# A two-block kernel on 272 columns: its first stage loads x in pieces, makes the parts of x straight from x, halves two weight slabs, issues zero products first and moves the statistic by some units

## The reference

```python
hn = rms_norm(h, g_mix[0])                      # h: meta tokens and x, 272 x 1024
z = hn @ w_in                                   # 1024 -> 384 + 256 + 32 + 3*512 + 8
c_q, c_kv, k_pe, fq, fk, fv, f_logit = split(z)
q = rms_norm(c_q, g_cq) @ w_uq ; kv = rms_norm(c_kv, g_ckv) @ w_ukv
qf, kf = rms_norm(fq per head, g_q_fox), rms_norm(fk per head, g_k_fox)
cum_log_f = cumsum(log_sigmoid(f_logit + b_forget))
# two attentions (one with cum_log_f as decay), joined @ w_out, then an MLP;
# after it a convolution mixer and MLP, then a second block of two mixers and two FFNs
```

## Time and profile before

| what | us |
|---|---|
| median of 3 runs | 1374.69 (1373.73 to 1377.56) |
| profiled execution, its own time | 1373.33 |
| its span | 1371.6 |
| TensorE busy (matmuls) | 1322.3 (96%) |
| DVE, ACT, POOL busy | 969.3, 735.5, 445.8 |
| first matmul | 12.79 |
| matmul of the statistic | 23.86 |
| first matmul of unit 2 | 24.22 |
| first matmul of unit 18 | 87.44 |
| first matmul of attention | 111.66 |

### The profile page before, as it was taken

One profiled execution on the slowest core, in us unless ns is written; L12 is line 12 of the kernel. 1 busy time (PEld: TensorE's weight loads), 2 busy tenths in 40 slices (PEclk: granted clock), 3 DMA queues, 4 the chain that ended last, 5 costly groups with the idle time before them and its releaser, 6 DMA issues. The chain is left out here.

```text
span 1371.6 us, 29146 instructions
## 1 busy us (share of the span) xinstructions
PE 1322.3 (96%) x10774; PEld 1288.3 (94%) x10774; DVE 969.3 (71%) x1440; ACT 735.5 (54%) x1204; POOL 445.8 (33%) x462
## 2 busy tenths in 40 slices
PE   5999999999999999999999999999999899999996
PEld 5787699999999999999989999999999889999996
DVE  6767567664578677655655569998569798999844
ACT  5454655444444444444455547665445785766642
POOL 3532044321111433311545423333125534343300
PEclk9998999999999999999999999999999999999998
DMA  7440044555545555555534555554554446555451
GB/s 268 166 141 32 1 152 159 184 185 183 184 181 189 180 184 184 185 184 183 205 134 155 185 185 185 183 183 145 201 207 154 154 162 208 185 184 183 147 198 54
DMA packets 34507, 230.52 MB, mean 168 GB/s; under 512 B 3838, under 2 KB 4990, under 8 KB 10662
## 3 DMA queue, kind: packets, MB, share of 16 engines
q1 hardware_dynamic: 33652, 226.47, 47.4%
q10 hardware_dynamic: 770, 2.90, 0.6%
HBM read 228.17 MB, written 1.05 MB: 167 GB/s over the span
## 5 line engine op out<-in xcount | busy, mean ns | idle before, releaser
L365 DVE TENSOR_TENSOR wlo<-raw,whi 128x1024 fp32r<-128x1024 f32 (+1 forms) x448 | 548.2, 1229 | 92.1 <-ACT whi L360 91.0
L400 PE MATMUL ps<-xhi,whi 128*128 128x256 f32 (+2 forms) x2064 | 585.0, 283 | 21.2 <-DVE wlo L365 17.8
L401 PE MATMUL ps<-xlo,whi 128*128 128x256 f32 (+2 forms) x2064 | 583.2, 283 | 0.0
L402 PE MATMUL ps<-xhi,wlo 128*128 128x256 f32 (+2 forms) x2064 | 581.9, 282 | 0.0
L360 ACT ACTIVATE whi<-raw 128x1024 fp32r<-128x1024 f32 (+1 forms) x448 | 448.9, 1009 | 134.1 <-PE ps L402 130.0
L400 PEld LDWEIGHTS ps<-xhi,whi 128*128 128x128 f32 x2064 | 390.2, 189 | 26.5 <-issue 20.8
L402 PEld LDWEIGHTS ps<-xhi,wlo 128*128 128x128 f32 x2064 | 390.9, 189 | 0.0
L401 PEld LDWEIGHTS ps<-xlo,whi 128*128 128x128 f32 x2064 | 388.5, 188 | 0.3
L400 PE MATMUL ps<-hhi,whi 128*128 128x256 f32 (+1 forms) x1184 | 335.2, 283 | 3.3 <-issue 2.6
L402 PE MATMUL ps<-hhi,wlo 128*128 128x256 f32 (+1 forms) x1184 | 334.4, 282 | 0.0
L401 PE MATMUL ps<-hlo,whi 128*128 128x256 f32 (+1 forms) x1184 | 334.2, 282 | 0.0
(11 more groups left out here) (261 smaller groups left out, 1293.2 us busy)
## 6 DMA issues: line engine op xcount, KB each, us to landing
raw<-w SPq DMA_DIRECT2D x184, 1024.0 KB, 4.8
raw<-w SPq DMA_DIRECT2D x40, 768.0 KB, 4.2
h<-x_fm ACTq DMA_DIRECT2D x1, 1088.0 KB, 6.3
out_fm<-h SPq DMA_DIRECT2D x8, 128.0 KB, 2.0
ws<-ws_src ACTq DMA_DIRECT2D x1, 512.0 KB, 4.6
bs<-bs_rows ACTq DMA_DIRECT2D x1, 512.0 KB, 5.4
consts<-constants ACTq DMA_DIRECT2D x1, 508.0 KB, 9.6
q_fox<-decay_rows SPq DMA_DIRECT2D x1, 340.0 KB
```

The costliest lines, as they stand in the source:

```text
L365: nc.vector.tensor_tensor(wlo[:, j % HLR, 0:n], raw[:, slot, col:col + n], whi[:, j % HLR, 0:n].bitcast(F32), ALU.subtract).then_inc(wlo_d ...
L400: nc.tensor.matmul(o, hi, xh, start=start, stop=False)
L401: nc.tensor.matmul(o, hi, xl, start=False, stop=False)
L402: mm = nc.tensor.matmul(o, lo, xh, start=False, stop=stop)
```

## The change

- x is loaded in 4 pieces of two chunks, each with its semaphore. `xhi` of even chunks is made by DVE, of odd chunks by ACT, straight from x times the gain; `xlo` by DVE in one instruction, x\*gain - xhi. `xg` is no longer used here.
- SP loads only the first 88 columns of params at first, the others after the pads (awaited after attention). Slab 0 is loaded in halves, the second issued once piece 1 of x is there; slab 1 in halves once all of x is there; then slab 2, `consts`, slab 3.
- TensorE first issues 46 products of zeros (128x128 by 256 columns, bank 7, operands in `chi`, cleared by DVE), then units 0 and 1 interleaved: hi\*hi and hi\*lo of unit 0, then of unit 1, then lo\*hi of both.
- The 8 squares go to 8 buffers; POOL sums them, after the last `xlo`. The column sum follows unit 4 instead of unit 1; root and reciprocal come at t = 3 and t = 4. ACT runs one Sqrt of a single column at the start.
- The shared tile is unit 4 instead of 0, the fox queries are units 0 to 3. The gate's first DVE steps are at t = 4 (were 1), the Exp at 5 (4), the reciprocal at 7 (5), the scan at 14 (12), the decay rows' DMAs at 16 (14).
- Spreads of the queries follow units 8 and 9 (were 7, 8), of the keys 12 and 13 (11, 12); the norms are at t = 9, 10 and 13, 14, and `inverse(1)` stands ahead of the norms of t = 10. `turn_v` is two groups after unit 14 (or query tile 2) and one a unit (or tile) later.

```diff
+WARM = 46
 # block.sync
-                    body(0, wait=False)
+                    half = UB * P
+                    sp.dma_start(raw[:, 0, 0:half], src[0][:, 0:half]).then_inc(s("unit0_loaded"), 16)
+                    sp.wait_ge(x_loaded[1], 16)
+                    sp.dma_start(raw[:, 0, half:cols], src[0][:, half:cols]).then_inc(raw_full[0], 16)
+                    for i in (0, 2, 3):
+                        sp.wait_ge(x_loaded[i], 16)
+                    sp.dma_start(raw[:, 1, 0:half], src[1][:, 0:half]).then_inc(s("unit2_loaded"), 16)
+                    sp.dma_start(raw[:, 1, half:cols], src[1][:, half:cols]).then_inc(raw_full[1], 16)
+                    sp.dma_start(raw[:, 2, 0:cols], src[2]).then_inc(raw_full[2], 16)
+                    sp.dma_start(consts[:, :], consts_in).then_inc(consts_in_done, 16)
+                    sp.dma_start(raw[:, 3, 0:cols], src[3]).then_inc(raw_full[3], 16)
+                    rest = pcol["conv_w"][0]
+                    sp.dma_start(params[:, rest:npar], params_in[:, rest:npar]).then_inc(s("params_loaded"), 16)
 # block.tensor
-            pe.wait_ge(consts_in_done, 16)
+            pe.wait_ge(s("warm_set"), 1)
+            for _ in range(WARM):
+                nc.tensor.matmul(ps[:, 7, 0:SEQ], chi[:, 0, 0:P], chi[:, 0, 0:SEQ], start=True, stop=True)
-                if u == 1:
+                if u == 4:
+                    pe.wait_ge(consts_in_done, 16)
+            def first_units():
+
+                o = [ps[:, take(), 0:T0] for _ in range(2)]
+                for u in range(2):
+                    pe.wait_ge(whi_done, u + 1)
+                    for b in range(8):
+                        if u == 0 and b % 2:
+                            pe.wait_ge(xhi_done, b + 1)
+                        elif u == 0:
+                            pe.wait_ge(xg_done, b + 2)
+                        nc.tensor.matmul(o[u], whi[:, u, b * P:(b + 1) * P], xhi[:, b, :], start=b == 0, stop=False)
+                    for b in range(8):
+                        if u == 0:
+                            pe.wait_ge(xlo_done, b + 1)
+                        nc.tensor.matmul(o[u], whi[:, u, b * P:(b + 1) * P], xlo[:, b, :], start=False, stop=False)
+                for u in range(2):
+                    pe.wait_ge(wlo_done, u + 1)
+                    for b in range(8):
+                        mm = nc.tensor.matmul(o[u], wlo[:, u, b * P:(b + 1) * P], xhi[:, b, :], start=False,
+                                              stop=b == 7)
+                    mm.then_inc(unit_done, 1)
+
+            first_units()
+            for u in range(2, U_KN):
-                if u in (7, 8):
+                if u in (8, 9):
                     for i in (0, 1):
-                        spread(0, 2 * (u - 7) + i, take_ring())
-                if u in (11, 12):
+                        spread(0, 2 * (u - 8) + i, take_ring())
+                if u in (12, 13):
                     for i in (0, 1):
-                        spread(1, 2 * (u - 11) + i, take_ring())
-                if u == 13:
-                    turn_v(1)
+                        spread(1, 2 * (u - 12) + i, take_ring())
+                if u == 14:
+                    turn_v(1, (0, 1))
+                if u == 15:
+                    turn_v(1, (2,))
-                    turn_v(0)
+                    turn_v(0, (0, 1))
+                if x == 3:
+                    turn_v(0, (2,))
 # block.vector
+            nc.vector.memset(chi[:, 0, :].bitcast(F32), 0.0).then_inc(s("warm_set"), 1)
+            for i in range(2):
+                first_xhi(2 * i)
+                first_xlo(2 * i)
+                first_xlo(2 * i + 1)
+            first_xhi(4)
+            first_xhi(6)
+            for kt in range(4, KT):
+                first_xlo(kt)
+            for j in range(LA):
                 split_lo(dve, 0, j, 8)
-            for kt in range(KT):
-                dve.wait_ge(sq_done, kt + 1)
-                dve.wait_ge(ssum_done, kt + 1)
-                nc.vector.tensor_tensor(ssum[:, :], ssum[:, :], sq[:, kt % 2, :], ALU.add).then_inc(ssum_done, 1)
-                if t in (8, 9):
-                    for i in (0, 1):
-                        fox_normed(0, 2 * (t - 8) + i)
                 if t == 10:
                     inverse(1)
+                if t in (9, 10):
+                    for i in (0, 1):
+                        fox_normed(0, 2 * (t - 9) + i)
+                if t == TL_PE:
+                    dve_rstd(dve, 0, 0, T0)
 # block.scalar
+            for i in range(4):
+                act.dma_start(h[:, 2 * i:2 * i + 2, :], x_in[:, 2 * i:2 * i + 2, :]).then_inc(x_loaded[i], 16)
+            act.wait_ge(s("warm_set"), 1)
+            nc.scalar.activation(four[:, 0:1], chi[:, 0, 0:1].bitcast(F32), ACT.Sqrt).then_inc(s("sqrt_ready"), 1)
+            first_xhi(1)
+            first_xhi(3)
+            act.wait_ge(s("unit0_loaded"), 16)
+            nc.scalar.activation(whi[:, 0, :], raw[:, 0, 0:UB * P], ACT.Copy).then_inc(whi_done, 1)
+            first_xhi(5)
+            first_xhi(7)
+            for j in range(1, LA + 1):
...
+                for kt in range(3 * j - 3, min(3 * j, KT)):
+                    nc.scalar.activation(first_sq[kt], h[:, kt, :], ACT.Square).then_inc(sq_done, 1)
...
+                if t == 3:
+                    act_root(act, 0, 0, T0)
 # block.gpsimd
+            pool.wait_ge(xlo_done, KT)
             for kt in range(KT):
-                pool_xlo(pool, 0, kt, kt % 2, 0, T0)
+                pool.wait_ge(sq_done, kt + 1)
+                pool.wait_ge(ssum_done, kt + 1)
+                nc.gpsimd.tensor_tensor(ssum[:, :], ssum[:, :], first_sq[kt], ALU.add).then_inc(ssum_done, 1)
```

More of the change, by code:

```diff
@@ L275, in program @@
         rows_loaded = sem("rows_loaded")
-        x_loaded = sem("x_loaded")
+        x_loaded = [sem(f"x_loaded{i}") for i in range(4)]
         raw_full = [sem(f"raw_full{i}") for i in range(RAW)]
@@ L752, in program @@
         pad_done = s("pad_loaded")
+        first_sq = [sq[:, 0, :], sq[:, 1, :], xg[:, 0, :], xg[:, 1, :], tmp[:, 0, :], tmp[:, 1, :], root[:, :],
+                    rstd[:, :]]
         vt_ps, vt_done = s("v_turned"), s("v_tok_done")
@@ L781, in _ @@
         def _(sp):
-            sp.dma_start(params[:, :], params_in).then_inc(small_in, 16)
+            first = pcol["conv_w"][0]
+            sp.dma_start(params[:, 0:first], params_in[:, 0:first]).then_inc(small_in, 16)
             def slabs(src, first, n, cols, rnd0):
@@ L835, in whole @@
                 bank = take()
[L836 removed]
                 mm = unit(pe, u // UB, u % UB, [(ps[:, bank, 0:T0], b == 0, b == 7) for b in range(8)],
[L838 removed]
+                          [x_rhs(b, 0, T0) for b in range(8)])
                 mm.then_inc(unit_done, 1)
[L840 removed]
+                if u == 4:
+                    pe.wait_ge(consts_in_done, 16)
                     pe_stats(pe, 0, 0, T0)
@@ L928, in turn_v @@
                     mm.then_inc(vt_ps, 1)
-            for u in range(0, U_KN):
+            def first_units():
[20 more added lines that the diff above has]
+            for u in range(2, U_KN):
                 whole(u)
@@ L1182, in _, with first_xhi, first_xlo @@
         def _(dve):
+            nc.vector.memset(chi[:, 0, :].bitcast(F32), 0.0).then_inc(s("warm_set"), 1)
             dve.wait_ge(small_in, 16)
-            dve.wait_ge(x_loaded, 16)
-            for kt in range(KT):
-                dve_gain(dve, 0, kt, kt % 2, 0, T0)
-                if kt == 4:
-                    split_lo(dve, 0, 0, 8)
-            for j in range(1, LA):
+            def first_xhi(kt):
+                dve.wait_ge(x_loaded[kt // 2], 16)
+                nc.vector.tensor_scalar(xhi[:, kt, :], h[:, kt, :], par(NORM_GAIN[0], kt), None,
+                                        ALU.mult).then_inc(xg_done, 2)
+            def first_xlo(kt):
+                if kt % 2:
+                    dve.wait_ge(xhi_done, kt + 1)
+                else:
+                    dve.wait_ge(xg_done, kt + 2)
+                nc.vector.scalar_tensor_tensor(out=xlo[:, kt, :], in0=h[:, kt, :], scalar=par(NORM_GAIN[0], kt),
+                                               in1=xhi[:, kt, :].bitcast(F32), op0=ALU.mult,
+                                               op1=ALU.subtract).then_inc(xlo_done, 1)
+            for i in range(2):
[7 more added lines that the diff above has]
+            for j in range(LA):
                 split_lo(dve, 0, j, 8)
-            for kt in range(KT):
-                dve.wait_ge(sq_done, kt + 1)
-                dve.wait_ge(ssum_done, kt + 1)
-                nc.vector.tensor_tensor(ssum[:, :], ssum[:, :], sq[:, kt % 2, :], ALU.add).then_inc(ssum_done, 1)
             nc.vector.memset(soft[:, :, :, :], 1.0).then_inc(s("soft_set"), 1)
@@ L1537, in _, with first_xhi @@
         def _(act):
-            act.dma_start(h[:, :, :], x_in).then_inc(x_loaded, 16)
```

(32 more changed lines are left out.)

50 lines of the change are left out of this document (27 added, 23 removed).

## The result

The changed kernel takes 1365.7 us in the median of five runs (1364.01 to 1368.24), the kernel before on the same chip 1374.69 (1373.73 to 1377.56): ratio 0.9935 [0.9921, 0.9949], 9.0 us less. Forecast were a time of 1362.7 and a gain of 12.0. The profiled execution took 1364.01 with a span of 1362.2, against 1373.33 and 1371.6.

The account below looks back on a forecast made before the run. TensorE, busy 96% of the span, was taken as the bound. Gains of 9.9 us at the start and 2.1 in waits sum to 12.0: 1373.33 to 1361.3, given as a median of 1362.7, range 1359.5 to 1368.0.

Parts of the forecast that it names:

- Loads: Start: DMAs move 0.43 MB a us, data landed 0.6 us after its last byte; unit 2 at 14.0, gain 9.9.
- no price for pieces: Loads at the start: splitting into pieces taken to cost nothing; 3.7 us more given as a middle.
- Rival B: Start: pieces load slowly, unit 2 starts 3.7 us later, time 1366.4; chance 0.10.
- First inverse: TensorE at the first query spread, near 38.5: wait for the inverse's low part 0.3 us in place of 1.84.
- Statistic: Column sum after unit 4: same 0.36 us, no wait; POOL's sums 0.74 to 0.8 each, 6 us of cover.
- Second pair, keys, transposes: After the first spread: new waits of 0.8 us for banks, 0.5 at the fourth spread, 0.4 at the transposes.
- Rival A: Start: clock rises late, all 46 zero products run slow, 3.1 us lost, time 1365.8; chance 0.12.
- Rival C: Up to attention: earlier TensorE only meets ACT and DVE; four new waits grow 1 us each, 1366.7; chance 0.10.
- The four waits: New TensorE waits before attention: 0.3 first inverse, 0.8 second pair, 0.5 fourth spread, 0.4 transposes; 2.0 us in all.
- Rival D: From the start: clock stays at 1.2 GHz, 2.4 us more a unit, 1401 if until unit 17; chance 0.03.
- Rival E: Past the start: something later runs at its own pace, the cut misses the end; within 0.3%, chance 0.05.

## Why the prediction came out as it did

The mechanism was right: but for the first inverse, TensorE's waits of before went as the forecast said, and the lead at attention's start is the lead at the end. 12.0 were forecast, 9.0 came. At attention's start the trace is 3.0 us behind the forecast: 2.3 at unit 2, 1.1 in the waits behind it, less 0.4 in small gaps that no row names.

- **Loads, the term that was mis-sized.** "So data counts as landed 0.6 us after its last byte" at 0.43 MB a us: the DMAs were taken to move at one rate, in order, but for a pause from 6.5 to 7.1. They moved 164 GB/s from 7 to 8, because SP had waited for pieces of x, and 238 to 264 until 12; and the half slab landed with 3.39 MB moved, not 2.8. The gain at unit 2 is 7.55, below the stated limits of 9.2 to 10.8. Those limits allowed 0.8 us for the half slab; it was 3.4 late.
- **The reason for taking no price for pieces** was a DMA share of 0.99. The same row has 180 GB/s. A full share says that the engines have packets under way, not what they move: it was 0.94 at 192 GB/s (pads, above), 1.04 at 343 and 1.01 at 428. With the pads the kernel before showed this already.
- **Rival B (pieces slow).** Its price of 3.7 was near the 3.4 by which the half slab was late, and its time of 1366.4 is nearer to the median than the forecast. In part that is luck: of the 3.0 us, 1.84 go with the pads (pads late), which B does not speak of, and x as one load gives back nothing that can be seen.
- **The Trainium skill** (DMA: Bandwidth & Descriptors, Bandwidth) had asked for 1 MB a DMA. The trace agrees in the direction, 343 to 360 GB/s with pieces against 428, and not in the size: x was whole by 8.1 us in four pieces and by 6.67 in one, so the pieces cost 1.4 us, where the estimate by that page had 8.1 us of transfer in place of 2.6. The estimate gives each piece the rate of a load that moves alone; here they were under way together with half a slab, at 343 to 360 GB/s in all.
- **First inverse: the step that failed.** The forecast had a wait of 0.3; it is 1.92. I followed SP's queue up to slab 3 and let slab 4 be there. Its issue waits for `wlo` 1 and stands behind two pads and a piece of params, and the DMAs are slow while these move. With the pads behind it the wait is 0.28.
- **Statistic.** Right that it costs no wait. The sums' price (0.8) was that of the short ones; five of eight took 1.43 to 1.74. Of the 6 us of cover (6.8 by the forecast's own marks) 2.4 were left.
- **Second pair, keys, transposes.** 0.55 for 0.8, 0.63 for 0.5, nothing for 0.4. The split of the transposes is worth some 2.2, the later spread some 4.4: more than the 1.7 and 1.8 that stand in the waits of before. For the spread the runs show why: the wait alone would be 3.31 on the earlier TensorE, and it then costs clock as well.
- **Rival A (late rise)** did not occur in the first trace: the zero products end at 8.3, and unit 0 runs at full pace. But the rise is not fixed. By the pace of the matmuls it comes 3.2 us after the first one in the kernel before, 5.1 with no zero products, and 3.3 to 5.9 after the first zero product in the eleven traces that have them; in the changed kernel itself 3.3 in one and 5.7 in the other. The Trainium skill (TensorE: Matmul & The Clock Gate, What's actually happening) says that this moment is not fixed to the kernel's start; the runs agree. Where it came late, the zero products ended at 9.4 and unit 2 had to wait for its `wlo` all the same, so the price of A was covered by the late slab.
- **Rival C (ACT and DVE no faster).** The four waits are 1.92, 0.55, 0.63 and 0, 1.1 more than forecast and not 4. The first of them alone is 1.6 over the forecast, and it came from a load, not from the pace of ACT or DVE.
- **Rival D (clock lost)** did not occur here, and its mechanism exists: after standing 3.3 us (spread early) and 3.87 (zeros alone) the clock was at half. It came back within 3.6 us each time, not after a whole stage.
- **Rival E:** the rest after attention's start is 1259.5 for 1259.9. Nothing is given back that a spread of 3.9 us between traces would let one see; the medians (9.0 less) agree with the 8.96 at attention.

The best versions measured are the changed kernel with the pads late, 1362.78, and that with contiguous halves as well, 1362.38; both ratios are about 0.9915. They lie 3 us below the changed kernel; the start of attention (1.8 and 2.3 earlier, with the wait for the inverse at 0.3 in each of the six traces that have late pads and the later spread) says so more firmly than the intervals of the ratios, which overlap.

Left open: why the DMA engines take until 12 us to fill after SP's waits end at 8.1, though five loads are issued by 10; why they move half as much beside the pads; which parts of the start carry the 5.5 us beside the halves of slab 1; and the 0.17% of the zero products alone.

## What to carry to other kernels

A wait on a DMA-issuing engine can be paid twice, as here: in the time that it holds back its own load, and in DMA engines that have run dry when the wait ends. Price it with both, and follow the issuing engine's queue two loads further than the last one you changed. Read the bytes per us beside the DMA share: here a full share went with half the rate. When TensorE gets earlier, every wait that was short before is longer by that lead less what moves with it, so shifting its consumers by a unit (some 4.4 us here) may be worth more than the row of the old wait says. Ask of each load not only how fast it comes but which bytes come first.
